# Start addresses of the buffers of split weights in a one-core mixer, attention and FFN trunk, from 1 KB multiples to four odd starts

## Time and profile before

| | before |
|---|---|
| median of 3 runs | 2194.74 us |
| the profiled execution | 2193.37 us |
| its span, first to last instruction | 2191.6 us |
| TensorE matmul busy | 2166.9 us, 99% |
| TensorE weight load busy | 1847.8 us, 84% |
| VectorE, ScalarE, GpSimd busy | 66%, 49%, 11% |
| granted TensorE clock | 0.998 |
| DMA | 393.83 MB, mean 180 GB/s |

### The profile page before, as it was taken

The page is one execution under the profiler, slowest core; times in us unless marked ns, Lnnn a source line. Parts: engine busy times, 40 slices in busy tenths (PEclk is TensorE's granted clock), DMA queues, the critical chain, the costliest instruction groups (busy, mean ns, idle before and its releaser), DMA issues.

```text
span 2191.6 us, 33212 instructions
## 1 busy us (share of the span) xinstructions
PE 2166.9 (99%) x12606; PEld 1847.8 (84%) x12606; DVE 1439.2 (66%) x1651; ACT 1065.0 (49%) x1438; POOL 244.6 (11%) x220
## 2 busy tenths in 40 slices
PE   8999999999999999999999999989999999999998
PEld 6888888788888888888888888878888888888887
DVE  7985658667554545467765544578777777876444
ACT  6452344545444444445444444566555555644443
POOL 1132000000000101025110001411111111100000
PEclk9999999999999999999999999999999999999999
DMA  7543344345666666675556543536555655566664
GB/s 265 177 150 115 119 146 157 129 157 185 193 192 192 192 192 191 193 265 182 187 180 198 190 151 122 189 118 206 187 182 194 188 190 181 193 191 212 193 192 152
DMA packets 107071, 393.83 MB, mean 180 GB/s; under 512 B 11888, under 2 KB 12144, under 8 KB 106576
## 3 DMA queue, kind: packets, MB, share of 16 engines
q1 hardware_dynamic: 106672, 391.10, 55.5%
q10 hardware_dynamic: 288, 1.18, 0.2%
HBM read 390.14 MB, written 2.10 MB: 179 GB/s over the span
## 4 chain that ended last, share of the span: by engine, by line
PE 94%; DVE 3%; ACT 1%; DMA 1%; issue 0%; SPq 0%; DVEq 0%; ACTq 0%
PE bank L1008 24%; PE bank L1017 13%; PE bank L543 7%; PE sm L430 5%; PE sm L429 5%; PE sm L427 5%; PE bank L546 4%; PE bank L1221 3%; PE bank L1223 3%; PE bank L1222 3%; PE bank L427 2%; PE bank L430 2%; PE bank L429 2%; PE sm L595 2%; PE bank L1105 1%; PE bank L1104 1%
## 5 line engine op out<-in xcount | busy, mean ns | idle before, releaser
L1977 DVE TENSOR_TENSOR part<-part,part 128x1024 fp32r<-128x1024 f32 x724 | 933.5, 1292 | 528.8 <-ACT part L1274 517.2
L1274 ACT ACTIVATE part<-part 128x1024 fp32r<-128x1024 f32 x724 | 763.7, 1057 | 579.2 <-PE sm L430 177.6
L1008 PE MATMUL bank<-part,part 128*128 128x512 f32 x2336 | 562.3, 392 | 0.0
L1008 PEld LDWEIGHTS bank<-part,part 128*128 128x128 f32 x2336 | 428.8, 188 | 83.1 <-issue 0.4
L1017 PEld LDWEIGHTS bank<-part,part 128*128 128x128 f32 x2336 | 300.0, 191 | 11.8
L1017 PE MATMUL bank<-part,part 128*128 128x256 f32 x2336 | 303.6, 283 | 0.0
L543 PE MATMUL bank<-part,part 128*128 128x512 f32 x832 | 207.3, 396 | 0.6 <-DVE part L2032 0.5
L427 PE MATMUL sm<-part,part 128*128 128x512 f32 x512 | 199.2, 389 | 0.0
L429 PE MATMUL sm<-part,part 128*128 128x512 f32 x512 | 199.2, 389 | 0.0
L430 PE MATMUL sm<-part,part 128*128 128x512 f32 x512 | 199.2, 389 | 0.0
L543 PEld LDWEIGHTS bank<-part,part 128*128 128x128 f32 x832 | 151.5, 188 | 32.9 <-issue 2.1
(11 more groups left out here) (382 smaller groups left out, 2203.5 us busy)
## 6 DMA issues: line engine op xcount, KB each, us to landing
part<-in_w_up SPq DMA_DIRECT2D x176, 512.0 KB, 4.5
part<-in_w_gate SPq DMA_DIRECT2D x128, 512.0 KB, 4.6
part<-in_w_dn SPq DMA_DIRECT2D x88, 512.0 KB, 4.4
part<-in_w_br SPq DMA_DIRECT2D x40, 512.0 KB, 4.6
part<-in_w_out SPq DMA_DIRECT2D x32, 512.0 KB, 4.6
part<-in_w_mk SPq DMA_DIRECT2D x32, 512.0 KB, 4.5
part<-in_w_mv SPq DMA_DIRECT2D x32, 512.0 KB, 4.5
part<-in_w_q SPq DMA_DIRECT2D x32, 512.0 KB, 4.4
```

The lines of the kernel that those rows point to most:

```text
L1008: mm = pe.matmul(dst, w[:, 0, k, :], x[:, k0 + k, :], start=start and k == 0, stop=stop and k == n - 1, skip_group_check=True)
L1274: act.activation(wsplit[(2 * m + h) % 4][:, 0, 0:n, :], raw[:, m % 2, h, 0:n, :], cp) .then_inc(sem("hi_done"), 1)
L1977: tt(w[:, 1, 0:n, :], raw[:, m % 2, h, 0:n, :], w[:, 0, 0:n, :].bitcast(f32), SUB).then_inc(sem("lo_done"), 1)
```

## The change

```
         region_at = -(-nc.sbuf_base // 1024) * 1024
         sb("gap", [P, (region_at - nc.sbuf_base) // 4])
+        ahead = (96, 64, 120, 112)
         sb("region", [P, REGION])
...
-        raw = part(0, 2, 2, 8, P)
-        wsplit = [partr(8192, 2, 8, P), partr(10240, 2, 8, P), partr(4096, 2, 8, P), partr(6144, 2, 8, P)]
+        raw = part(-192, 2, 2, 8, P)
+        wsplit = [partr(a - n, 2, 8, P) for a, n in zip((8192, 10240, 4096, 6144), ahead)]
         H = partr(12288, KT, 2 * T)
```

## The result

The changed kernel takes 2214.39 us, the median of four runs (2213.74 to 2216.96), against 2194.22 for the kernel before beside it. The ratio is 1.0093, with a 95% interval of 1.0075 to 1.0110: 20 us slower. The forecast was no change. Its range (2150 to 2228) holds the time, and the slower rival's 2218 is near it, but only in small part for that rival's reason, as the experiments show.

A forecast was written before the change was run, and what follows sets the result against it. The prediction took the distance between TensorE's matmul starts as the bound. Moves of `raw`, the splits and the split matmuls summed as 0 + 0 + 0, so 2194.7 us, unchanged, with a range of 2150 to 2228.

The forecast's parts named there:

- slower rival: Split matmuls: each change of buffer disturbs TensorE's rhythm, 0.034 us each, 23 to 24 us together, 2218; chance 27%.
- What bounds the kernel: Whole kernel: time can change only in the distance between matmul starts on TensorE, some 10,000 times over.
- cost of `raw`'s move: SyncE's DMAs writing `raw`: transfers land in 4.5 us with time to spare, so cost 0.
- third term: All 9984 split matmuls at other addresses: 0 taken, between no price and L503's, which gives 2239 or 2259.
- first reason: Split matmuls: relative starts already differ by multiples of 512 bytes without effect, so no pattern over 512 bytes is at work.
- second reason: Split matmuls: a pattern below 512 bytes would mostly average out, as the operands run past each other within one matmul.
- Its third: FFN matmuls: TensorE keeps 3.65 us per 16 while VectorE, ScalarE and DMAs use the same buffers more or less.
- The row that could decide nothing: L503, stationary operand moving 240 bytes per matmul: 233 ns mean, taken as bound from above, 44 us on 512-column matmuls.
- The excess: Split matmuls, faster case: time a changed start might remove; one buffer of four, up to 40% of it, within 2150.
- faster rival: Split matmuls: the collision of the two operand reads is real and depends on the start; chance 31%.
- Its sign: FFN, slower rival: the 16 matmuls of L1008 take over 3.68 us, with a bump at the ninth.

The follow-up runs named there:

- raw_only: Kernel before with only `raw` started 768 bytes earlier, the split buffers left at multiples of 1 KB; 2193.73 us, ratio 0.9998.
- uniform kernels: Changed kernel with one start for all four split buffers, 384, 256, 480 or 448 bytes ahead of the old; ratios 1.0132, 1.0001, 1.0148, 1.0020.
- all_256: Changed kernel with all four split buffers 256 bytes ahead of their old starts; 2193.90 us, ratio 1.0001 to the kernel before.
- all_480: Changed kernel with all four split buffers 480 bytes ahead of their old starts; 2225.84 us, ratio 1.0148 to the kernel before.
- region_480: Kernel before with the whole region, activations and split buffers alike, moved 480 bytes ahead; 2193.93 us, ratio 0.9997.
- low_64_behind: Kernel before with high parts kept at multiples of 256 bytes and only the low parts put 64 bytes behind; 2206.54 us, ratio 1.0057.
- all_448: Changed kernel with all four split buffers 448 bytes ahead of their old starts; 2198.05 us, ratio 1.0020 to the kernel before.
- mixed kernels: Changed kernel with two split buffers 480 bytes ahead, two at multiples of 256, in two orders; 2212.87 and 2211.32 us, ratios 1.0085 and 1.0079.
- by_form: Chunks used feature-major split 64 bytes ahead of a multiple of 256, those used token-major at the multiple; 2185.89 us, ratio 0.9962 to the kernel before.

## Why the prediction was wrong, point by point

- **What bounds the kernel**: right. Only the distances between matmul starts could move, and they account for all of the 20 us. TensorE stayed busy 99% of the span. VectorE's split (1291 ns for 1292), ScalarE's (1058 for 1057) and the DMAs (4.5 us to landing, as before) kept their times, and `raw_only` (2193.73 us) shows the cost of `raw`'s move to be 0, as put.
- **The step that failed** is the third term, "Between those ends I take 0": the price of other addresses in the split matmuls, put at nothing, measured 20 us, of which the distances of the uniform kernels make 16.5. Its first reason was right and was carried too far: the distances by multiples of 512 bytes made no difference (3.65 us per 16 with `H` and with `X1`), and 256 ahead didn't either (`all_256`, 2193.90 us), but the change is about what lies below. Its second reason, that a shorter pattern averages out since the operands run past each other, is refuted by `all_480` (233.3 ns instead of 226.6 in the gates, on every matmul). Its third, the 3.65 us that hold while the other engines and the DMAs use the same buffers more or less, speaks of those other users alone. `region_480` (2193.93 us) beside `all_480` (2225.84) shows that the distance of TensorE's own two operands counts: token-major 226.8 ns at 0, 233.3 at 480 ahead. What in TensorE or in the memory causes it, no run here shows.
- **The row that could decide nothing** is L503. I took its 230, 230 and 240 ns as a sign that odd distances gain nothing, and their mean of 233 as a bound from above. The mean is near what 32, 128 or 224 bytes cost in the table, but nothing shows that the distance made it. The four matmuls of each group stand behind matmuls of another shape, and at distance 0 such a start is slow too. In the kernel before, the second and third distances of the FFN's 16 are 236 and 228 ns before 227 is reached, and a group of 8 from L543, close to L503, takes 230 ns each (start us, us):

```profile
262.10 1.84 PE bank L543 x8
```

  The second and third distances of L503's eight groups, from the starts of the matmuls and not of the weight loads, have a mean of 231.4 ns, where 236 and 228 at distance 0 have 232. So its row can't be told from a slow start alone, and it spoke neither for the 0 nor for a price.
- **The excess** of which the range and the faster rival speak was my estimate, and no run shows this term: no trace tells which part of a split matmul's time could go. What the runs showed in its place is the least mean of each kind over all layouts: 228.7 ns (`low_64_behind`) and 226.8 (the kernel before) for 512 columns, feature-major and token-major, and 114.5 (`all_448`) for 256. Attention's 215.6 ns (3.45 us for 16 matmuls) belong to 256 float32 columns, another shape and another type; no layout's mean for 512 split columns came down to them.
- **The faster rival** is wrong for this change, but a part of it exists: at 448 ahead the 256-column matmuls take 114.5 ns, 5.3 less than before, and one buffer of the four has that distance.
- **The slower rival** had the time (2218 for 2214) mostly by luck. It priced each change of buffer at 0.034 us, 24 us in all, and the distance itself at nothing. The uniform layouts show 16.5 us for the distances; what is left for changes is some 4 us. A change cost about 0.02 us token-major and 0.0035 in the 512-column runs of the mixed kernels. Its sign, over 3.68 us for the 16 matmuls of L1008, came (3.70 and 3.72), but `all_480` shows 3.73 with no change anywhere, so that sign could not tell it from a price of distance.

## What to carry to other kernels

If TensorE is the bound and its matmuls read float32r operands, as here, the distance of the stationary from the moving operand is worth a trial: it moved this kernel from 0.4% under to 1.9% over the aligned layout. Put both at the same remainder modulo 256 bytes first, then try the other remainders with one value for all buffers and read the distance between matmul starts for each shape apart. A small group behind matmuls of another shape, as L503, doesn't show by itself what a change of addresses will cost: compare it first with an equally short group at the old distance. That no effect is seen between aligned layouts, as here between multiples of 512 bytes, is no evidence about unaligned ones.

## What the runs showed of the hardware that I had not expected

- The time of this kernel's float32r matmuls depends on the distance of their two operands modulo 256 bytes, 226.8 to 234.3 ns for 512 columns token-major, and not on the start of both together: moving both by 480 bytes left every mean as it was (`region_480`, 228.8, 119.8 and 226.8 ns). The period of 256 rests on two layouts, `all_256` and `by_form`.
- The best distance differed by shape: 512 columns had their lowest means at 0 (228.8 and 226.8 ns), 256 columns had 114.5 ns at 192 ahead and 116.3 at 64, for 119.8 at 0.
- A mixture of distances within a group of three matmuls cost 5.2 ns on each of them (`low_64_behind`, 232.0 for 226.8), though one of the two distances has 226.8 alone and the other 228.9.
- Behind matmuls of another shape, this kernel's feature-major ones of 512 columns took five distances (233, 236, 228, 232 and 231 ns in the kernel before) until they settled at 226.7.
